# The forget gate's sums in the attention scores: rounded matmuls over 128 rows in place of four-byte matmuls of 8 rows

## The chip, the cores and the metric

The kernel runs on one core of a Trainium2 chip, in one launch. The metric is the time of that launch on the device in microseconds (us); lower is better. Before the change the runs gave 3453.53 us as their median, from 3452.12 to 3457.21 (3 runs).

## The reference

The reference is a block of two layers over 512 tokens of 1024 features: first a mixer with a recurrent unit and a convolutional feed-forward part, then a state space branch, a "forgetting" attention and a feed-forward part that picks 16 of 16384 experts for each of 8 heads and token. Only the attention is touched here:

```
def forgetting_attention(q, k, v, f_logit, f_bias, q_g, k_g):
    q = head_rms_norm(q...); k = head_rms_norm(k...)
    log_f = jax.nn.log_sigmoid((f_logit + f_bias).astype(jnp.float32)).transpose(0, 2, 1)
    cum = jnp.cumsum(log_f, axis=-1)
    ...
        s = jnp.einsum('bhqd,bhkd->bhqk', q_blk, k).astype(jnp.float32) * scale
        s = s + c_blk[..., None] - cum[:, :, None, :]
        s = jnp.where(key_pos[None, :] <= q_pos[:, None], s, -jnp.inf)
        p = jax.nn.softmax(s, axis=-1)
        return jnp.einsum('bhqk,bhkd->bhqd', p.astype(v.dtype), v)
```

There are 8 heads of 128 features and 4 blocks of 128 queries. The term `c_blk` is the same for all keys of a query and drops out of the softmax, so a kernel only has to add `-cum` of the key to each score.

## The kernel before, in words

The program is written engine by engine, and the order on each engine is the order of the code; semaphores tie them together. Every activation lies with features on the 128 partitions and tokens along the columns. Weights stream through a ring of 5 tiles of 128x1024 (`fetch`, on SyncE). A projection is computed with operands in two parts: ScalarE rounds a tile to the type fp32r (`high`, L930), VectorE or GpSimd subtracts to get the rest (`low`, L1310 and L1962), and TensorE runs three rounded matmuls of 512 columns for each of 8 chunks (`three`), 24 in all. An fp32 operand instead makes four-byte matmuls, which the trace shows as two passes each with its own weight load. All matmuls are recorded under the helper line L576, transposes under L837.

The attention part on TensorE: the last two projections of keys, the 8-row projection `f` of the forget gate, the values `vv`, then `scores(0)`, and a loop over heads `hd` = 0 to 7, here called rounds: a projection (`k2` to `k7`, then `ga6`, `ga7`), the transposes of the probabilities, for rounds 0 to 5 a `head_sum` (the sum of squares of the new keys, for their norm), `scores(hd + 1)`, and the product of probabilities and values ("mixing", `probsT,vt`). So `scores` is called 8 times, as call 0 ahead of the loop and as call n in round n - 1.

A call of `scores` handles 4 blocks of queries; block qb has (qb + 1) x 128 keys. Each block is a sum of three products in one bank of PSUM: keys and queries (`kT`, `qT`); `sel` and `cumn`, which adds row hd of the 8x512 sums to all 128 queries; and `ident` and `maskt`, which puts -1e30 above the diagonal of the last 128 columns. All three are four-byte. The lower four banks are used in turn by head sums and score blocks. With five of them in rounds 0 to 5, the last block of a call takes the bank of the head sum in front of it, and waits for ScalarE's square root of that sum (`hsd_done`).

Beside it ScalarE evicts the projection (to `kT` or `gaT`), rounds the next weight tile, squares the keys (`ht`), rounds `mg` of the head before once VectorE has merged it, takes the root of the head sum, computes the exponentials of the four blocks, and evicts the mixed values. VectorE makes the weight tile's low half, merges the head before (L1802, L1803), copies the transposed probabilities `probsT` (L1815), takes the maxima of the score blocks (L1784), norms the new keys (L1703, L1704) and divides the probabilities by their sums (L1791, L1792, "the shares"), which the next round's transposes wait for.

The forget gate's sums are made by VectorE between the `f` projection and the work for `vv` (L1761 to L1771): `cumn` is 8x512. GpSimd builds `sel` (a one in row hd for head hd, 128 columns wide) once the states are done.

Of the kernel before, what the change touches and what calls it, by code (L numbers as in the profile page):

```python
# [15 lines left out]
P = 128  # L16
# [236 lines left out]
def build(nc, io):  # L253
    with ExitStack() as ctx:
# [7 lines left out]
        def sb(name, cols, dt=F32):  # L262
            return ctx.enter_context(nc.sbuf_tensor(name, [P, cols], dt))
# [2 lines left out]
        wh_t, wl_t = sb("wh", RH * D, F32R), sb("wl", RH * D, F32R)  # L266
        vec, mod_t, small = sb("vec", NVEC), sb("mod", 96), sb("small", 1024)
        ones, ident, iota, maskt = sb("ones", P), sb("ident", P), sb("iota", P), sb("mask", P)
        ARENA = 39400
        base = 4 * (-(-nc.sbuf_base // 32) * 8)  # L270
        sb("arena", ARENA)
# [2 lines left out]
        def ar(name, at, chunks, w=T, dt=F32):  # L274

            assert at + chunks * w <= ARENA
            t = nc.alloc_sbuf_tensor_at(name, [P, chunks * w], dt, offset=base + 4 * at)
            return t[:, :].rearrange("p (c w) -> p c w", w=w)
# [67 lines left out]
        gl = ar("gl", B + 20480, 4)  # L346
        kT, vt2 = ar("kT", B, HEADS), ar("vt2", B + 12288, NB, D)
        fl = [ar(f"fl{k}", B + 20480 + k * T, 1)[0:HEADS, 0, :] for k in range(5)]
        sel, cumn = ar("sel", B + 23040, HEADS, P), ar("cumn", B + 24064, 1)[0:HEADS, 0, :]
        probs = [ar(f"probs{k}", B + 20480 + k * (k + 1) // 2 * P, 1, (k + 1) * P)[:, 0, :] for k in range(NB)]  # L350
        probsT = [ar(f"probsT{k}", B + 21760 + (k * NB - k * (k - 1) // 2) * P, 1, (NB - k) * P)[:, 0, :]
                  for k in range(NB)]
# [91 lines left out]
        def _(sp):  # L444
# [6 lines left out]
            def stream(stage, name, n, w=D):  # L451
                for u in range(n):
                    fetch(TILE[f"{stage}{u}"], io[name][u], w)
# [66 lines left out]
                projection(f"k{n}")  # L520
            fetch(TILE["f"], io["w_f"], KD * HEADS)
            stream("vv", "w_v2", 8)
            for name in IN_HEADS:
                projection(name)
            stream("out2_", "w_out2", KD)
# [46 lines left out]
        def _(pe):  # L572
# [244 lines left out]
            def scores(hd):  # L817
                pe.wait_ge(S("qk_normed"), HEADS + hd + 1)
                for qb in range(NB):
                    b, nk = BLOCK[f"scores{hd}"] + qb, (qb + 1) * P  # L820
                    block_free(pe, b)
                    mm(bank(b, nk), qT[:, hd, qb * P:(qb + 1) * P], kT[:, hd, 0:nk], True, False)
                    mm(bank(b, nk), sel[0:HEADS, hd, :], cumn[:, 0:nk], False, False)
                    mm(bank(b)[:, qb * P:nk], ident[:, :], maskt[:, :], False, True).then_inc(PE, 1)

            pe.wait_ge(S("cum_ready"), 1)
            pe.wait_ge(S("mask_ready"), 2)
            scores(0)
            pe.wait_ge(S("v2_read"), 2 * NB)
            for hd in range(HEADS):  # L830
# [468 lines left out]
        def _(ve):  # L1299
# [454 lines left out]
            for n in range(2):  # L1754
# [13 lines left out]
            log1p_exp(fl[1], fl[3], fl[4], fl[3], fl[2])  # L1768
            link(TS(fl[1], fl[0], 0.0, -1.0, ALU.min, ALU.mult))
            link(TT(fl[2], fl[2], fl[1], ALU.add))  # L1770
            v.tensor_tensor_scan(cumn, ones[0:HEADS, 0:1].to_broadcast([HEADS, T]), fl[2], 0.0, ALU.mult, ALU.add)\  # L1771
                .then_inc(S("cum_ready"), 1)
            for n in range(2):
                low_after(TILE[f"vv{n}"])
                head_norm(HEADS + n)
# [167 lines left out]
        def _(gp):  # L1943
# [10 lines left out]
            g.affine_select(out=maskt[:, :], in_=maskt[:, :], compare_op=ALU.is_ge, fill=NEG, base=0,  # L1954
                            pattern=[[-1, P]], channel_multiplier=1).then_inc(S("mask_ready"), 1)

            def low(name):

                e = HALF[TILE[name]]
                wh, wl = whl(e, 0, D)  # L1960
                gp.wait_ge(S("high_ready"), e + 1)
                g.tensor_tensor(wl, slot(WHOLE_OF[e], 0, D), wh.bitcast(F32), ALU.subtract)\  # L1962
                    .then_inc(S("low_by_gp"), 1)
            for name in FFN:
                if name[0] != "d":
                    low(name)

            gp.wait_ge(S("out_done"), NS)
            g.memset(sel, 0.0).then_inc(S("mask_zero"), 1)
            gp.wait_ge(S("mask_zero"), 2)  # L1970
            g.affine_select(out=sel, in_=sel, compare_op=ALU.not_equal, fill=1.0, base=0,
                            pattern=[[-1, HEADS], [0, P]], channel_multiplier=1).then_inc(S("mask_ready"), 1)

            for j in range(PK):
                low(f"ui{j}")
# [123 lines left out]
```

## Time and profile before

| | us |
|---|---|
| median of the runs | 3453.53 |
| the profiled execution | 3455.41 |
| its span, first to last instruction | 3452.9 |
| TensorE matmuls busy | 3306.8 (96%) |
| VectorE busy | 2017.2 (58%) |
| ScalarE busy | 1076.0 (31%) |
| GpSimd busy | 428.3 (12%) |

The granted TensorE clock over the span is 0.98 of full. The chain of work that ended last lies 88% on TensorE and 9% on VectorE.

How to read it: an engine is "busy" from the start to the end of its instructions; those of TensorE overlap, and their ends are modelled, so the distance from one start to the next tells more than a duration. In a timeline a row may stand for several instructions merged ("x2"). The idle time before a row and what ended it stand in brackets. The attention part lies between about 1516 and 1730 us.

### The profile page before, as it was taken

How to read it: one execution, taken by the hardware profiler on the slowest of the kernel's cores; microseconds unless marked ns; L12 is line 12 of the kernel's file. 1: busy time of each engine (PE TensorE's matmuls, PEld its weight loads, DVE VectorE, ACT ScalarE, POOL GpSimd, SP SyncE). 2: the span in 40 equal slices, each digit the busy share in tenths (PEclk: the TensorE clock that was granted, in tenths of full speed). 3: DMA queues.
4: the chain of work that ended last, by engine and by line, in shares of the span. 5: the costliest groups of instructions: out<-in, count | busy, mean ns of one | idle time of the engine just before them, and what ended most of it. 6: DMA issues, size and time to landing. Idle time of an engine off the chain costs nothing.

```text
span 3452.9 us, 37952 instructions
## 1 busy us (share of the span) xinstructions
PE 3306.8 (96%) x14700; PEld 2589.5 (75%) x14700; DVE 2017.2 (58%) x3757; ACT 1076.0 (31%) x1401; POOL 428.3 (12%) x184
## 2 busy tenths in 40 slices
PE   7999889989999699999989999999999999999999
PEld 6776678867777455766568888888888788888887
DVE  5678443347897789644633858676641255555554
ACT  3265222223223222224432333355542211111111
POOL 0000000003132000000001344432334200000000
PEclk9999999999999899999999999999999999999999
DMA  5144214332242333221123344387875555555553
GB/s 187 47 142 128 86 61 139 116 100 80 80 153 75 108 119 107 86 74 55 31 61 95 127 139 140 126 196 185 197 189 195 177 190 187 187 191 184 192 185 116
DMA packets 280946, 451.56 MB, mean 131 GB/s; under 512 B 147776, under 2 KB 154048, under 8 KB 280512
## 3 DMA queue, kind: packets, MB, share of 16 engines
q1 hardware_dynamic: 145152, 405.10, 36.1%
q10 hardware_dynamic: 135616, 44.04, 6.0%
q8 instruction: 117, 1.92, 0.2%
q14 instruction: 61, 0.50, 0.0%
HBM read 369.39 MB, written 79.69 MB: 130 GB/s over the span
## 4 chain that ended last, share of the span: by engine, by line
PE 88%; DVE 9%; ACT 2%; issue 1%; DMA 0%; ACTq 0%; DVEq 0%
PE psum L576 88%; DVE wl L1310 1%; DVE ht L1703 1%; ACT wh L930 1%; DVE st L1712 1%; DVE n L1455 0%; DVE yb L1513 0%; DVE h_lo L1449 0%; DVE trig L1404 0%; DVE lb L1504 0%; DVE st L1719 0%; DVE st L1722 0%; DVE cs L1511 0%; DVE trig L1405 0%; DVE trig L1407 0%
## 5 line engine op out<-in xcount | busy, mean ns | idle before, releaser
L576 PE MATMUL psum<-h_hi,wh 128*128 128x512 f32 x2144 | 872.8, 407 | 44.6 <-DVE h_lo L1449 21.0
L1310 DVE TENSOR_TENSOR wl<-ring,wh 128x1024 fp32r<-128x1024 f32 (+2 forms) x320 | 375.1, 1175 | 887.4 <-ACT wh L930 887.0
L576 PE MATMUL psum<-h_lo,wh 128*128 128x512 f32 x2144 | 850.2, 397 | 0.0
L576 PE MATMUL psum<-h_hi,wl 128*128 128x512 f32 x2144 | 849.9, 396 | 0.0
L930 ACT ACTIVATE wh<-ring 128x1024 fp32r<-128x1024 f32 (+2 forms) x492 | 504.1, 1027 | 851.9 <-PE psum L576 839.1
L1962 POOL TENSOR_TENSOR wl<-ring,wh 128x1024 fp32r<-128x1024 f32 x172 | 424.7, 2470 | 1942.6 <-ACT wh L930 1942.6
L576 PEld LDWEIGHTS psum<-h_hi,wh 128*128 128x128 f32 x2144 | 406.0, 189 | 150.0 <-issue 43.6
L576 PEld LDWEIGHTS psum<-h_hi,wl 128*128 128x128 f32 x2144 | 406.0, 189 | 102.6
L576 PEld LDWEIGHTS psum<-h_lo,wh 128*128 128x128 f32 x2144 | 406.7, 190 | 91.9 <-issue 4.1
L576 PE MATMUL psum<-ews_hi,wh 128*128 128x512 f32 x1024 | 408.7, 399 | 0.7 <-ACT ga L1280 0.7
L576 PE MATMUL psum<-ews_hi,wl 128*128 128x512 f32 x1024 | 403.5, 394 | 0.0
L576 PE MATMUL psum<-ews_lo,wh 128*128 128x512 f32 x1024 | 401.4, 392 | 0.0
L1280 ACT ACTIVATE ga<-psum 128x512 f32<-128x512 f32 x128 | 76.5, 597 | 501.1 <-PE psum L576 501.1
L576 PEld LDWEIGHTS psum<-ews_hi,wl 128*128 128x128 f32 x1024 | 192.2, 188 | 50.1
L576 PEld LDWEIGHTS psum<-ews_lo,wh 128*128 128x128 f32 x1024 | 192.2, 188 | 45.9
L576 PEld LDWEIGHTS psum<-ews_hi,wh 128*128 128x128 f32 x1024 | 192.2, 188 | 45.3 <-ACT ga L1280 1.1
L1905 DVE TENSOR_SCALAR hot_a<-psum,picksT 128x128 f32<-128x128 f32 x512 | 173.8, 401 | 0.0
L1901 DVE TENSOR_TENSOR hot_b<-psum,picksT 128x512 f32<-128x512 f32 x128 | 87.5, 684 | 116.6 <-PE psum L576 116.6
L1646 DVE SCALAR_TENSOR_TENSOR psum<-ffpad,vec,psum 128x512 f32<-128x512 f32 x176 | 133.1, 756 | 6.3
L1916 DVE TENSOR_TENSOR er<-abuf,gbuf 128x512 f32<-128x512 f32 x128 | 90.0, 703 | 70.6 <-DMA gbuf<-gates_scratch 70.6
L1267 ACT ACTIVATE stage<-psum 128x512 f32<-128x512 f32 x128 | 126.1, 1124 | 3.3 <-PE psum L576 2.0
L576 PEld LDWEIGHTS psum<-hot_b,hot_a 128*128 128x128 f32 x1024 | 120.9, 192 | 3.6
(357 smaller groups left out, 3852.3 us busy)
## 6 DMA issues: line engine op xcount, KB each, us to landing
ring<-tables SPq DMA_DIRECT2D x256, 512.0 KB, 3.7
acts_scratch<-ga SPq DMA_DIRECT2D x128, 256.0 KB, 2.2
gates_scratch<-stage ACTq DMA_DIRECT2D x8, 4096.0 KB, 27.1
abuf<-acts_scratch SPq DMA_DIRECT2D x128, 256.0 KB, 3.9
gbuf<-gates_scratch SPq DMA_DIRECT2D x128, 256.0 KB, 4.2
ring<-w_up SPq DMA_DIRECT2D x44, 512.0 KB, 3.6
ring<-w_modb SPq DMA_DIRECT2D x32, 512.0 KB, 3.7
statew<-states_scratch SPq DMA_DIRECT2D x16, 640.0 KB, 3.8
```

The costliest lines, as they stand in the source:

```text
L576: return nc.tensor.matmul(out, lhsT, rhs, start=first, stop=last, **kw)
L930: A(whl(e, 0, size[t])[0], slot(t, 0, size[t]), ACT.Copy).then_inc(S("high_ready"), 1)
L1267: A(parked[g % 2][:, :, t0:t0 + 4].rearrange("p j t -> p t j"), t3(bank(b), P), ACT.Copy)\
L1280: A(ga4[:, j % 4, :], psum[:, 4 + j % 2, :], ACT.Gelu_apprx_tanh).then_inc(S("ea_ready"), 1)
L1310: TT(wl, slot(t, 0, size[t]), wh.bitcast(F32), ALU.subtract).then_inc(S("low_by_ve"), 1)
L1646: step(STT(cv, win, C("fcw", n * 9 + k), cv, ALU.mult, ALU.add))
L1703: link(v.reciprocal(ht[:, 2 + n % 2, :], ht[:, 2 + n % 2, :]))
L1712: TT(st[:, k, :], psum[:, bk, :], tab, ALU.mult).then_inc(S("xs_read"), 1)
L1901: TT(t3(hot_b[:, n % 4, :], P), rows.unsqueeze(1).to_broadcast([P, 4, P]), picksT[:, 1, 4 * n:4 * n + 4].unsqueeze(2).to_broadcast([P, 4, ...
L1905: last = TS(hot_a[:, n % 4, q * P:(q + 1) * P], rows, picksT[:, 0, t:t + 1], picksT[:, 2, t:t + 1], ALU.is_equal, ALU.mult)
L1916: TT(er[:, b % 2, :], abuf[:, b % NV, :], gbuf[:, b % NV, :], ALU.mult).then_inc(S("ew_raw"), 1)
L1962: g.tensor_tensor(wl, slot(WHOLE_OF[e], 0, D), wh.bitcast(F32), ALU.subtract)\
```

## The change

`sel` and the four-byte use of `cumn` go. The 8x512 sums are kept in two rounded parts: `cums` is a tile of 128 rows of which rows 0 to 7 hold the rounded sums and rows 32 to 39 the rounded rest; all other rows are zero. VectorE writes the rounded part and the rest (into `cum_lo`, rows 0 to 7), and a DMA on SyncE moves the rest to rows 32 to 39. The stationary operand is a column of `pick_head`, which has a one in rows hd and 32 + hd, read 128 times over. One rounded matmul then adds both parts. The mask goes through rounded copies of `ident` and `maskt`. The product of keys and queries stays as it is.

```
-        sel, cumn = ar("sel", B + 23040, HEADS, P), ar("cumn", B + 24064, 1)[0:HEADS, 0, :]
+        ident_r, mask_r = sb("ident_r", P, F32R), sb("mask_r", P, F32R)
+        pick_head = sb("pick_head", HEADS, F32R)
+        cums, cum_lo = (ar(name, B + at, 1, T, F32R)[:, 0, :] for name, at in (("cums", 23040), ("cum_lo", 23552)))
+        cumn = ar("cumn", B + 24064, 1)[0:HEADS, 0, :]
...  (SyncE, behind the fetches of w_v2)
             stream("vv", "w_v2", 8)
+            sp.wait_ge(S("cum_ready"), 1)
+            sp.dma_start(cums[32:32 + HEADS, :].bitcast(F32), cum_lo[0:HEADS, :].bitcast(F32)).then_inc(S("cum_moved"), 16)
...  (TensorE, scores)
                     mm(bank(b, nk), qT[:, hd, qb * P:(qb + 1) * P], kT[:, hd, 0:nk], True, False)
-                    mm(bank(b, nk), sel[0:HEADS, hd, :], cumn[:, 0:nk], False, False)
-                    mm(bank(b)[:, qb * P:nk], ident[:, :], maskt[:, :], False, True).then_inc(PE, 1)
-
-            pe.wait_ge(S("cum_ready"), 1)
-            pe.wait_ge(S("mask_ready"), 2)
+                    mm(bank(b, nk), pick_head[:, hd:hd + 1].to_broadcast([P, P]), cums[:, 0:nk], False, False)
+                    mm(bank(b)[:, qb * P:nk], ident_r[:, :], mask_r[:, :], False, True).then_inc(PE, 1)
+
+            pe.wait_ge(S("cum_moved"), 16)
+            pe.wait_ge(S("mask_ready"), 4)
             scores(0)
...  (VectorE, after the scan's input)
-            v.tensor_tensor_scan(cumn, ones[0:HEADS, 0:1].to_broadcast([HEADS, T]), fl[2], 0.0, ALU.mult, ALU.add)\
-                .then_inc(S("cum_ready"), 1)
+            link(v.tensor_tensor_scan(cumn, ones[0:HEADS, 0:1].to_broadcast([HEADS, T]), fl[2], 0.0, ALU.mult, ALU.add))
+            ve.wait_ge(S("cum_zero"), 1)
+            link(v.tensor_copy(cums[0:HEADS, :], cumn))
+            TT(cum_lo[0:HEADS, :], cumn, cums[0:HEADS, :].bitcast(F32), ALU.subtract).then_inc(S("cum_ready"), 1)
...  (GpSimd, at the start)
+            gp.wait_ge(S("consts_ready"), 4)
+            gp.wait_ge(S("mask_ready"), 1)
+            g.tensor_copy(mask_r[:, :], maskt[:, :]).then_inc(S("mask_ready"), 1)
+            g.tensor_copy(ident_r[:, :], ident[:, :]).then_inc(S("mask_ready"), 1)
+            g.tensor_tensor(pick_head[:, :], ident[:, 0:HEADS], ident[:, 32:32 + HEADS], ALU.add)\
+                .then_inc(S("mask_ready"), 1)
...  (GpSimd, behind out_done)
-            g.memset(sel, 0.0).then_inc(S("mask_zero"), 1)
-            gp.wait_ge(S("mask_zero"), 2)
-            g.affine_select(out=sel, in_=sel, compare_op=ALU.not_equal, fill=1.0, base=0,
-                            pattern=[[-1, HEADS], [0, P]], channel_multiplier=1).then_inc(S("mask_ready"), 1)
+            g.memset(cums.bitcast(F32), 0.0).then_inc(S("cum_zero"), 1)
```

On TensorE the order stays, with other operands. This is one call of `scores` in a round of the changed kernel, with the semaphores that each row waits for:

```order
L581 MATMUL psum<-ht,ones 128x512 [waits hsq_ready,p_exp]
L581 MATMUL psum<-kT,qT 128x128 [waits p_exp,qk_normed]
L581 MATMUL psum<-cums,pick_head 128x128
L581 MATMUL psum<-mask_r,ident_r 128x128
L581 MATMUL psum<-kT,qT 128x256 [waits p_exp]
L581 MATMUL psum<-cums,pick_head 128x256
L581 MATMUL psum<-mask_r,ident_r 128x128
L581 MATMUL psum<-kT,qT 128x384 [waits p_exp]
L581 MATMUL psum<-cums,pick_head 128x384
L581 MATMUL psum<-mask_r,ident_r 128x128
L581 MATMUL psum<-kT,qT 128x512 [waits hsd_done]
L581 MATMUL psum<-cums,pick_head 128x512
```

Each pair of `cums` and `mask_r` stands where `cumn` and `mask` stood; the waits are those of before.

On SyncE, the queue around the fetches of the values' weights, before:

```order
L449 DMA ring<-w_f 128x64 [waits low_by_ve]
L449 DMA ring<-w_v 128x1024 [waits low_by_ve] x4
L449 DMA ring<-w_v 128x1024 [waits pe_done]
L449 DMA ring<-w_v 128x1024 [waits low_by_ve] x3
L449 DMA ring<-w_k 128x1024 [waits low_by_ve] x6
```

and of the changed kernel:

```order
L452 DMA ring<-w_f 128x64 [waits low_by_ve]
L452 DMA ring<-w_v 128x1024 [waits low_by_ve] x4
L452 DMA ring<-w_v 128x1024 [waits pe_done]
L452 DMA ring<-w_v 128x1024 [waits low_by_ve] x3
L527 DMA cums<-cum_lo 8x512 [waits cum_ready]
L452 DMA ring<-w_k 128x1024 [waits low_by_ve] x6
```

The move of the rest stands ahead of the fetches of the keys' weights.

## Rows read from the trace of the kernel before

**Rows 1.** The page: an engine's busy us, share of the span, instructions

```profile
PE 3306.8 (96%) x14700; PEld 2589.5 (75%) x14700; DVE 2017.2 (58%) x3757; ACT 1076.0 (31%) x1401; POOL 428.3 (12%) x184
```

**Rows 2.** The chain that ended last: start, us, TensorE's piece in two rounds

```profile
1668.57 17.32 PE psum L576 x58
1688.12 15.64 PE psum L576 x58
```

**Rows 3.** By tile, `cumn`: ns min/median/max, first and last start, forms

```profile
L576 PE MATMUL psum<-cumn,sel x64: 270/480/692, 1581.1 to 1710.6; 8*128 8x128 f32 x16, 8*128 8x256 f32 x16, 8*128 8x384 f32 x16, 8*128 8x512 f32 x16
```

**Rows 4.** Timeline of call 1 on TensorE: start, us, engine, line, operation

```profile
1598.06 0.39 PE L576 MATMUL psum<-kT,qT 128*128 128x128 f32 x2
...
1603.45 1.12 PE L576 MATMUL psum<-cumn,sel 8*128 8x512 f32 x2
1604.50 0.49 PE L576 MATMUL psum<-mask,ident 128*128 128x128 f32 x2
1604.82 2.32 PE L576 MATMUL psum<-probsT,vt 128*128 128x512 f32 x8
```

**Rows 5.** Timeline of round 1, all engines; idle time in brackets

```profile
1612.58 1.25 PE L837 MATMUL psum<-ident,probs 128*128 128x128 f32 x10
...
1614.98 1.10 PE L576 MATMUL psum<-ht,ones 128*128 128x512 f32 x2 [1.15 <-ACT ht L1164]
...
1615.91 0.39 PE L576 MATMUL psum<-kT,qT 128*128 128x128 f32 x2
...
1616.94 1.69 DVE L1815 COPY probsT<-psum 128x512 f32<-128x512 f32 x4
...
1618.88 0.69 ACT L1150 ACTIVATE ht<-psum,vec 128x512 f32<-128x512 f32 x1
...
1620.35 1.02 PE L576 MATMUL psum<-kT,qT 128*128 128x512 f32 x2
...
1622.68 2.32 PE L576 MATMUL psum<-probsT,vt 128*128 128x512 f32 x8
...
1629.10 0.49 DVE L1792 TENSOR_SCALAR probs<-probs,small 128x512 f32<-128x512 f32 x1
```

**Rows 6.** Timeline of an early projection on TensorE, 512 and 256 columns

```profile
102.18 0.39 PE L576 MATMUL psum<-h_lo,wh 128*128 128x512 f32 x1
...
102.65 0.28 PE L576 MATMUL psum<-hc_hi,wh 128*128 128x256 f32 x1
102.77 0.28 PE L576 MATMUL psum<-hc_lo,wh 128*128 128x256 f32 x1
```

**Rows 7.** Timeline around call 0: TensorE, then ScalarE

```profile
1580.80 0.38 PE L576 MATMUL psum<-kT,qT 128*128 128x128 f32 x2
...
1587.61 0.77 PE L576 MATMUL psum<-h_hi,wh 128*128 128x512 f32 x1
...
1594.72 1.25 PE L837 MATMUL psum<-ident,probs 128*128 128x128 f32 x10
...
1582.02 2.04 ACT L1215 ACTIVATE vt<-psum 128x512 f32<-128x512 f32 x4
```

**Rows 8.** Stretches: busy us (count) of five engines, then clock, DMA, GB/s

```profile
1555.00:1580.50 25.50, 22.35 (x96) 17.98 (x96) 5.75 (x5) 6.18 (x8) 0.00 (x0) 1.00 0.33 102
...
1587.50:1591.00 3.50, 3.50 (x11) 2.78 (x11) 2.52 (x9) 0.78 (x2) 0.00 (x0) 0.53 0.00 0
1675.00:1680.00 5.00, 5.00 (x11) 2.55 (x12) 3.32 (x2) 1.73 (x6) 0.00 (x0) 0.66 0.00 0
```

**Rows 9.** Timeline of round 6: VectorE and TensorE

```profile
1707.96 1.68 DVE L1815 COPY probsT<-psum 128x512 f32<-128x512 f32 x4
...
1711.45 2.32 PE L576 MATMUL psum<-probsT,vt 128*128 128x512 f32 x8
```

**Rows 10.** Timeline of VectorE around the gate's sums

```profile
1542.43 0.68 DVE L1770 TENSOR_TENSOR fl<-fl,fl 8x512 f32<-8x512 f32 x1
...
1544.29 1.19 DVE L1310 TENSOR_TENSOR wl<-ring,wh 128x1024 fp32r<-128x1024 f32 x1
```

## The prediction

> **What bounds the kernel now.** I read the busy shares first: TensorE is busy for 3306.8 us, 96% of the span [rows 1]. Anything on TensorE that is not covered by a wait elsewhere is time. Then the stretch of the change: the attention part calls `scores` eight times, once in front of the loop over heads and once inside each of its first seven rounds. The rows by tile show that the sums of the forget gate run as 64 matmuls with an 8-row stationary operand, two passes for each of 32 matmuls [rows 3]; the mask has as many. The timeline of one `scores` call shows what they take [rows 4]: it runs from 1598.06 to 1604.82, 6.76 us. In its last block of 512 columns the sums take 1603.45 to 1604.50 = 1.05 us and the mask 1604.50 to 1604.82 = 0.32 us. Last the timeline of one round [rows 5], to see which wait comes last there, and the granted clock [rows 8].
>
> **The matmuls, one call.** Four blocks of 128, 256, 384 and 512 columns, each with three products. The product of keys and queries stays four-byte. Its columns are those of the `probsT,vt` matmuls, also four-byte with 128 rows: two passes over 1280 columns in 2.32 us [rows 4], whose last one is drawn some 0.2 us long past the next start. So 1.2 columns per ns, 2 x 1280 / 1.2 = 2.13 us. Within the call now it takes more: sums in proportion to 1.05 us (two passes, plus about 0.2 us of weight loads that start only with the matmul) come to 0.41 + 0.63 + 0.84 + 1.05 = 2.93 us, the mask to 4 x 0.32 = 1.28 us, so 6.76 - 4.21 = 2.55 us is left for keys and queries. I take the difference of 0.42 us for the cost of switching between 8 and 128 rows, and let it go.
>
> The rounded form's cost is read from the projections [rows 6]: two products of 512 columns take 102.65 - 102.18 = 0.47 us, 0.235 each, one of 256 columns 0.12 us, one pass. 384 columns lie between, 0.18. 128 columns in this form are in no row. Below stands 128 / 512 of 0.235, 0.06; above, the two passes of the mask now, 0.32. Nearest are ten transposes of 128 columns with a load each, 1.25 us in all, at most 0.125 each [rows 5]. I take 128 / 1.2 = 0.107, a load's time at that pace. Sums: 0.11 + 0.12 + 0.18 + 0.23 = 0.64. Mask: 0.43. The call comes to 2.13 + 0.64 + 0.43 = 3.2 us, 3.5 less than now. If the loads stay exposed and the 128-column products cost twice my value, it is 2.55 + 0.75 + 0.86 = 4.2 us, 2.6 less. Four bytes of `cums` in 128 rows instead of 8 cost TensorE nothing by columns. The stationary operand of the sums reads one column 128 times over; no row shows such a load. From below it costs what other loads do; from above I allow one pass more per product, which the 4.2 us holds in part.
>
> **Where the gain is let through.** *Call 0, ahead of the loop* [rows 7]: starts at 1580.80, would end at 1584.0. The projection behind it waits for ScalarE's four copies of `vt`, 1582.02 + 2.04 = 1584.06. It starts at about 1584.2 in place of 1587.61: 3.4 us.
>
> *Call 1, in round 0*: nothing waits inside (round 0 has no merge of a head before, so ScalarE's root of the head sum comes some 2 us earlier than in a later round), so 3.5 us.
>
> *Calls 2 to 6, in rounds 1 to 5* [rows 5]: here a new wait appears. The head sum and the four score blocks use four banks, so that the last block needs the bank of the head sum in front of it, and waits for `hsd_done`, ScalarE's root of that sum. That root is at 1618.88 + 0.69 = 1619.57 and stands behind a copy that waits for VectorE's merge, so it hangs on the start of the round and not on the scores. Now TensorE comes to the last block at 1620.35, later than the root. After, the first three blocks take 2.0 us from 1615.91, to 1617.9, and TensorE waits to about 1619.7 (the root and some 0.1 us for the signal). The last block takes 0.853 + 0.234 + 0.107 = 1.2 us: end 1620.9 to 1621.0 in place of 1622.68, 1.7 us a round, 5 x 1.7 = 8.5 us. Half of the saved work turns into that wait. It also covers dear small products in the first three blocks, up to 1.8 us.
>
> Does another wait come late next? The mixing product wants `probsT`, whose copies start at 1616.94 and take 1.69: there before 1619. The next round's transposes want the shares, now at 1629.10 + 0.49 = 1629.59, against their turn one round after 1612.58, at 1612.58 + (1612.58 - 1594.72) = 1630.44 [rows 5, 7]: 0.85 us to spare. That VectorE chain (last maximum, norm of the keys, the shares) starts from the last score block, and moves earlier by the same 1.7 us, so the 0.85 us stay.
>
> *Call 7, in round 6* [rows 9]: no head sum, no such wait. The call ends at 1711.45 - 3.5 = 1707.95, but `probsT` is copied only from 1707.96 on; its first copy is out near 1708.6. Gain 1711.45 - 1708.6 = 2.85 us. Round 7 has no scores, and its waits follow the end of its projection, so nothing is given back.
>
> Sum: 3.4 + 3.5 + 8.5 + 2.85 = 18.2 us.
>
> **The clock.** Twice in this part the granted clock falls to its lower level, 1.2 of 2.4 GHz, while TensorE is busy all the time: 0.53 in 1587.5 to 1591, behind call 0, and 0.66 in 1675 to 1680, in a round [rows 8]. Both follow `scores`. A wait of 3.15 us in the stretch from 1555 left it at 1.00 [rows 8]. The projection behind call 0 took 1594.72 - 1587.61 = 7.1 us against 24 x 0.235 = 5.6 at full clock, 1.5 us more; the round took 17.32 against 15.64 in its sister at 1688.12 [rows 2], 1.7 us more. What goes away is 8-row work, what comes is work on 128 rows and 1.8 us of waiting a round, less than the 3.15 us that the clock bore. I expect both drops to go: 3.2 us, and 0 to 3.2 as bounds, with up to 3 lost instead if the new waits bring drops.
> The Trainium skill's "TensorE: Matmul & The Clock Gate" (Part 1, what is actually happening) puts a drop down to idle time of TensorE. The trace does not bear that out for these two, where it was busy throughout. By that rule the change removes no cause and adds waits, so the sum would stay at 18.2 us or less; this is the second case below.
>
> **What lies beside other work.** VectorE gets a copy and a subtraction of 8x512, at most 0.68 us each as the addition of that shape, and a few hundredths between [rows 10]. Queued behind them is the low half for a weight tile three ahead, at 1544.29, which TensorE reaches two projections later; a shift of 1.4 us is hidden by the projections in between (5.6 us each), and if it were not it would cost at most that. The sums' low part then moves by DMA to rows 32 to 39, 16 KB. SyncE waits for `cum_ready` before it; behind stands the fetch of the next `w_k` tile, which waits for the low half that VectorE makes after the sums anyway. The transfer has from about 1546 to 1580.80 to land, so TensorE's wait for it is free; a move that took 50 us would cost some 16. GpSimd has three small operations at the start and later one memset in place of two operations, all far from use.
>
> **Sum.** 18.2 + 3.2 = 21.4 us. The profiled execution took 3455.4 us, 1.9 more than the median of the runs, 3453.53. That gives 3434.0, or 3432.1 against the median; I say 3433.
>
> **Rivals.**
> 1. The clock drops stay, or the new waits make others: 18.2 less, 3436 (down to 3439 with more drops). For: drops come and go with phase, and only two of eight calls had one. Against: both stood behind work that goes. Chance 0.25.
> 2. Dear small products: the call saves only 2.6 us. Calls 0, 1 and 7 lose 0.9 each (call 7 0.3), rounds 1 to 5 about 0.3 each, 3.6 in sum: 3437. For: 128 columns in this form are in no row. Against: one pass cannot well cost what two do. Chance 0.12.
> 3. The wait for the head sum's root does not bind (TensorE's bank is free earlier than I read): rounds 1 to 5 give 3.5 each, 9 more, 3424. For: nothing in a row, as it doesn't wait now. Against: the wait stands in the order, and the root's time is in the trace. Chance 0.04.
> 4. Slower: going over between four-byte and rounded products, or the load of a repeated column beside it, stops TensorE for p us. There are 8 changes of form in a call, 64 in all. In rounds 1 to 5 the wait swallows 1.8 us of the six ahead of the last block. Cost: 64 p - 5 x 1.8. It decides from (21.4 + 9) / 64 = 0.48 us each; at 0.6 us it is 3434 + 29.4 = 3463. For: no row has such a sequence. Against: the score call at 1580.80 and the transposes at 1612.58 are four-byte work straight behind rounded projections, with no idle time ahead of them [rows 5, 7]. Chance 0.04.
> 5. The change does not do what it says: with a four-byte product in the same sum, the rounded ones run at four-byte pace. Only the exposed loads go, 0 to 3 us: 3453. Against: the form is the operands' own, as in the projections. Chance 0.05.
>
> The forecast itself has 0.50 and runs from 3429 to 3435.5. Over all cases the range is 3427 to 3441. A difference under 0.2%, 7 us, can hardly be told from none: faster 0.91, same 0.05, slower 0.04.
>
> **What would show it.** `cums,pick_head` once for each block, 0.23 us apart at 512 columns; calls of about 3.2 us; a TensorE wait of 1.8 us on ScalarE's root before the last block of calls 2 to 6 and none in the others; rounds of about 16.1 us; clock 1.00 through the part. Calls over 4.5 us, a wait for `cum_moved`, or transposes waiting for the shares would make it wrong.

## The result and the profile after

| | before | changed |
|---|---|---|
| median of the runs, us | 3455.33 (3452.12 to 3457.21, 4 runs) | 3425.61 (3424.03 to 3427.22, 4 runs) |
| profiled execution, us | 3455.41 | 3424.04 |
| its span, us | 3452.9 | 3422.1 |

The changed kernel takes 0.9915 of the time before, 95% interval 0.9898 to 0.9932: 29.7 us less. The forecast was 3433, with 3427 to 3441 as its range, so the kernel came out 1.4 us below the range's lower end. (The median before is over one run more than the 3453.53 that the forecast started from.) The direction and the work on TensorE were right; the sum lacked some 8 us.

The page of the changed kernel, its line of the engines [rows 1]:

```profile
PE 3267.0 (95%) x14636; PEld 2587.9 (76%) x14636; DVE 2018.4 (59%) x3759; ACT 1076.3 (31%) x1401; POOL 429.2 (13%) x186
```

64 matmuls are gone: 32 passes of the sums and 32 of the mask. The rows by tile, `cums`, with ns min/median/max [rows 3, 10]:

```profile
L581 PEld LDWEIGHTS psum<-cums,pick_head x32: 190/190/192, 1577.1 to 1684.4; 128*128 128x128 f32 x32
L581 PE MATMUL psum<-cums,pick_head x32: 305/550/800, 1577.1 to 1684.4; 128*128 128x128 f32 x8, 128*128 128x256 f32 x8, 128*128 128x384 f32 x8, 128*128 128x512 f32 x8
...
L1778 DVE CAST cums<-cumn x1: 415/415/415, 1538.0 to 1538.0; 8x512 fp32r<-8x512 f32 x1
L1779 DVE TENSOR_TENSOR cum_lo<-cumn,cums x1: 679/679/679, 1538.4 to 1538.4; 8x512 fp32r<-8x512 f32 x1
L527 SPq DMA_DIRECT2D cums<-cum_lo x1: 759/759/759, 1539.2 to 1539.2; - x1
```

One pass for each block, and the load of a column read 128 times over takes 190 ns, as those of `probsT,vt` do. VectorE's two new instructions take 1.1 us; the move to rows 32 to 39 was issued at 1539.2, long before its use at 1577.

The timeline of call 1 on TensorE, after [rows 4]:

```profile
1589.29 0.38 PE L581 MATMUL psum<-kT,qT 128*128 128x128 f32 x2
...
1591.28 1.07 PE L581 MATMUL psum<-kT,qT 128*128 128x512 f32 x2
1591.79 0.80 PE L581 MATMUL psum<-cums,pick_head 128*128 128x512 f32 x1
1592.43 0.22 PE L581 MATMUL psum<-mask_r,ident_r 128*128 128x128 f32 x1
1592.48 1.07 PE L581 MATMUL psum<-probsT,vt 128*128 128x512 f32 x2
```

The call takes 1592.48 - 1589.29 = 3.19 us in place of 6.76. (Single rows inside it can't be added up: their ends are modelled, and starts follow them.)

The timeline of round 1, after [rows 5]:

```profile
1600.27 1.25 PE L842 MATMUL psum<-ident,probs 128*128 128x128 f32 x10
...
1603.91 0.69 DVE L1810 SCALAR_TENSOR_TENSOR mg<-mg,gaT 128x512 f32<-128x512 f32 x1
...
1604.64 0.63 ACT L1240 ACTIVATE mg_hi<-mg 128x512 fp32r<-128x512 f32 x1 [2.10 <-DVE mg L1810]
...
1605.29 1.28 ACT L1155 ACT_TABLE_LOAD   x1
...
1606.58 0.69 ACT L1155 ACTIVATE ht<-psum,vec 128x512 f32<-128x512 f32 x1
...
1607.32 1.12 PE L581 MATMUL psum<-kT,qT 128*128 128x512 f32 x2 [1.56 <-ACT ht L1155]
...
1608.58 2.37 PE L581 MATMUL psum<-probsT,vt 128*128 128x512 f32 x8
```

The new wait stands before the last block of the call, for ScalarE's root of the head sum, and in front of the root stand a table load of 1.28 us and the copy that waits for VectorE's merge. The chain that ended last now runs through it, in each of rounds 1 to 5:

```profile
1603.91 0.71 DVE mg L1810
1604.66 0.09 issue
1604.77 0.52 issue
1605.29 1.28 ACT L1155
1606.58 0.70 ACT ht L1155
1607.28 0.04 issue
1607.32 9.23 PE psum L581 x36
```

**Where the time went.** Turns, that is the starts of `ident,probs` of a round, put against those of before:

| stretch | before, us | after, us | gain | forecast |
|---|---|---|---|---|
| up to call 0's start | 1580.80 | 1576.95 | 3.85 | 0 |
| call 0 and the projection behind it | 13.92 | 9.00 | 4.92 | 4.9 |
| round 0 | 17.86 | 14.32 | 3.54 | 3.5 |
| rounds 1, 2, 3, 5 | 17.86 each | 16.11 each | 1.75 each | 1.7 each |
| round 4 | 19.55 | 16.11 | 3.44 | 3.4 |
| round 6 | 15.61 | 13.01 | 2.60 | 2.85 |
| behind the last turn | 1733.7 | 1728.3 | 5.4 | 0 |

From call 0 to the last turn the kernel gained 21.5 us; the forecast for it was 21.4. All that it missed, 9.3 us of the two profiled executions, lies outside: the early and late stages hold no changed instruction of TensorE, and yet they were faster. The stretch 2600 to 3300 of both, filled by the experts' matmuls (busy us and count of TensorE, weight loads, VectorE, ScalarE, GpSimd, then clock, DMA share, GB/s); before:

```profile
2600.00:3300.00 700.00, 699.31 (x2997) 562.27 (x2996) 311.85 (x421) 144.18 (x149) 50.52 (x21) 1.00 0.56 186
```

and after:

```profile
2600.00:3300.00 700.00, 699.31 (x3009) 566.68 (x3009) 328.98 (x442) 141.89 (x144) 39.13 (x17) 1.00 0.56 189
```

Both at full clock, with no idle time to speak of, and 12 matmuls more after. From start to start a rounded matmul of 512 columns takes 233.33 ns before and 232.38 after (mean over the experts' stages). What differs for them is where their tiles lie: the three new tiles hold 264 words in each partition, and stand ahead of the arena in which all activations lie, so it moved by 1056 bytes. (Words here are 4 bytes, and all shifts are in each partition.) The kernel has 11,040 such matmuls, 4128 of them ahead of 1550 us and some 6600 behind the attention part; 0.95 ns each would be 10.5 us, 3.9 ahead and 6.3 behind.

### The profile page after: what moved, and what is told of

Its sections match the earlier page's. It is cut to its first block, busy times and chain, and to the rows that moved or that the text cites. A ratio compares the mean times of both kernels' runs of the same rounds, so it can differ in the third digit from the quotient of the medians.

```text
span 3422.1 us, 37830 instructions
## 1 busy us (share of the span) xinstructions
PE 3267.0 (95%) x14636; PEld 2587.9 (76%) x14636; DVE 2018.4 (59%) x3759; ACT 1076.3 (31%) x1401; POOL 429.2 (13%) x186
## 4 chain that ended last, share of the span: by engine, by line
PE 87%; DVE 9%; ACT 2%; issue 1%; DMA 0%; ACTq 0%; DVEq 0%
PE psum L581 87%; DVE wl L1315 1%; ACT wh L935 1%; DVE ht L1708 1%; DVE st L1717 1%; DVE n L1460 0%; DVE yb L1518 0%; DVE h_lo L1454 0%; DVE trig L1409 0%; DVE lb L1509 0%; DVE st L1724 0%; DVE st L1727 0%; DVE cs L1516 0%; DVE trig L1412 0%; DVE trig L1410 0%
```

## The experiments

Kernels that ran together share runs of the kernel before, whose median lay between 3455.1 and 3456.0. Ratios are against it.

### The place of the arena

**1 and 2. The kernel before, its arena moved by 264 words, and by 8.**

```
+        sb("unused", 264)          # in the second: 8
         sb("arena", ARENA)
```

> The kernel before with one unused tile of 264 words a partition ahead of the arena, which is what the three new tiles of the change take: the arena starts 1056 bytes later, nothing else changes. Theory PLACE (the rounded matmuls' pace hangs on where their operands in the arena start; 233.3 ns a piece before and 232.4 after in the expert stage): this kernel shows the 232.4 ns and is some 9 us faster than the kernel before, near 3446. Rival RUN (the pace is of the execution or the chip, not of the program): no change from the kernel before, 3455.

> The kernel before with an unused tile of 8 words (32 bytes) ahead of the arena. By the sizes of the tiles the arena starts at 32 bytes past a multiple of 64 before, and at a multiple of 64 after the change (1056 = 16 x 64 + 32). Theory PLACE in the form 'it is the 64-byte phase': the same 9 us as with 264 words, near 3446, at 232.4 ns. If PLACE holds in another form (a bank, a larger distance), this kernel stays at 3455 while the one with 264 words moves. Theory RUN: 3455 for both.

Measured: 3445.00 us (0.9968, interval 0.9956 to 0.9981) and 3443.46 (0.9964, 0.9950 to 0.9977), both at 232.38 ns. An unused tile ahead of the arena is worth 10 to 12 us, and 32 bytes do as much as 1056. 1056 is 32 more than a multiple of 128.

**3. The changed kernel, its arena moved by 8 words more.**

> The changed kernel with an unused tile of 8 words (32 bytes) ahead of the arena, which puts it back to 32 bytes past a multiple of 64. Theory PLACE by the 64-byte phase: the rounded matmuls go back to 233.3 ns and the kernel loses some 9 us, 3434 to 3435. Theory RUN: 3425.6 as the changed kernel.

Measured: 3444.62 (0.9966, 0.9952 to 0.9980): 19 us slower than the changed kernel, 10 slower than I expected. The same stretch has 24 matmuls fewer than in the changed kernel, 234.28 ns each:

```profile
2600.00:3300.00 700.00, 699.31 (x2985) 562.21 (x2985) 319.66 (x430) 141.72 (x145) 45.22 (x19) 1.00 0.55 186
```

Theory PLACE in its 64-byte form fell with that: there are not two paces but three at least.

**4. The changed kernel with its three tiles behind the arena.** The arena lies where it lay before.

```
-        ident_r, mask_r = sb("ident_r", P, F32R), sb("mask_r", P, F32R)
-        pick_head = sb("pick_head", HEADS, F32R)
         ARENA = 39400
...
         sb("arena", ARENA)
+        ident_r, mask_r = sb("ident_r", P, F32R), sb("mask_r", P, F32R)
+        pick_head = sb("pick_head", HEADS, F32R)
```

> The changed kernel with its three new tiles behind the arena instead of ahead of it, so that the arena starts where it did before: the change of the matmuls alone. Theory PLACE, in any form: 3434, which is the kernel before less the 21.4 us of the prediction's sum. Theory RUN: 3425.6.

Measured: 3433.41 (3433.11 to 3433.68; 0.9935, 0.9922 to 0.9949), with rounds of 14.32, 16.11 five times, 13.04:

```profile
2600.00:3300.00 700.00, 699.31 (x2998) 562.27 (x2997) 324.73 (x436) 142.30 (x145) 41.72 (x18) 1.00 0.56 187
```

This is the change alone, at the pace of before, and what the forecast of 3433 spoke of.

**9, 10, 13 and 14. Which shift sets the pace.** 9: the kernel before, arena moved by 16 words. 10: the changed kernel, arena moved by 16 words more. 13: the kernel before, 8 unused words ahead of all tiles, so that weights and arena move by 32 bytes together. 14: weights moved by 32 bytes and the arena by 128.

```
+        sb("unused", 8)            # 13 and 14, ahead of wh and wl
         wh_t, wl_t = sb("wh", RH * D, F32R), sb("wl", RH * D, F32R)
...
+        sb("unused2", 24)          # 14
         sb("arena", ARENA)
```

> The kernel before with an unused tile of 16 words (64 bytes) ahead of the arena. So far the rounded matmuls of the expert stage ran at 233.3 ns with the arena in the old place, 232.4 at +32 and +1056 bytes, 234.3 at +1088. Theory PHASE128 (the pace hangs on the arena's start modulo 128 bytes, as 1056 = 8 x 128 + 32 and 1088 = 8 x 128 + 64): +64 bytes runs like +1088, 234.3 ns, and is as much slower as the changed kernel was between those places (3444.6 - 3433.4 = 11.2 us): 3466. Rival DISTANCE (1088 bytes moved something by its size, not by its phase): 3455 or 3445.

> The changed kernel with 16 unused words ahead of the arena: it starts 1120 = 8 x 128 + 96 bytes past the old place, the fourth phase of 32 bytes. Theory PHASE128 says that it has a pace of its own, and not which. By the three known (0: 233.3, 32: 232.4, 64: 234.3 ns) I expect it between the two neighbours 64 and 0, 233.3 to 234.3 ns: 3433 to 3445. Rival, the 64-byte phase counts in part: 232.4 ns as at 32, 3425.6.

> The kernel before with 8 unused words (32 bytes) ahead of all its tiles: the weights' ring, the rounded weights wh and wl, and the arena with the moving operands all start 32 bytes later. Theory MOVING (the pace hangs on where the moving operand in the arena starts, absolutely): as with the arena alone 32 bytes later, 232.4 ns and 3443.5. Theory RELATIVE (it hangs on the distance of the two operands, which stays): 233.3 ns and 3455. A third pace would say that both places count.

> The kernel before with 8 unused words ahead of all tiles and 24 more ahead of the arena: ring, wh and wl start 32 bytes later, the arena 128 bytes later, which is its old phase. Theory MOVING: 233.3 ns and 3455, as before. Theory RELATIVE: the distance changes by -32 modulo 128, as with the arena at +96 alone: 233.3 ns by that kernel too, so here the two agree; theory STATIONARY (the weights' place counts): another pace, and a time that differs by 5 us or more.

Measured, ordered by the arena's shift less that of the weights, modulo 128 bytes. This is the distance of the two operands counted from the kernel before, where it is called 0. (The ns are means from start to start over the experts' stages.)

| distance | kernel | weights, arena moved (bytes) | ns | time, us | ratio (interval) |
|---|---|---|---|---|---|
| 0 | before | 0, 0 | 233.33 | 3455.33 | |
| 0 | 13 | 32, 32 | 233.33 | 3454.69 | 1.0001 (0.9992 to 1.0010) |
| 0 | 4 | 0, 0 | 233.34 | 3433.41 | 0.9935 (0.9922 to 0.9949) |
| 32 | 1, 2 | 0, 1056 / 0, 32 | 232.38 | 3445.00 / 3443.46 | 0.9968 / 0.9964 |
| 32 | changed | 0, 1056 | 232.38 | 3425.61 | 0.9915 (0.9898 to 0.9932) |
| 64 | 9 | 0, 64 | 234.28 | 3462.74 | 1.0020 (1.0011 to 1.0029) |
| 64 | 3 | 0, 1088 | 234.28 | 3444.62 | 0.9966 (0.9952 to 0.9980) |
| 96 | 10 | 0, 1120 | 233.33 | 3433.31 | 0.9935 (0.9922 to 0.9949) |
| 96 | 14 | 32, 128 | 233.33 | 3453.24 | 0.9994 (0.9985 to 1.0003) |

Experiment 13 moved the arena by the 32 bytes that gave experiment 2 its 12 us, and gained nothing: it is not the place of the arena alone. In 14 the arena has moved by a full 128 bytes and the weights by 32. By the mean, 233.33 ns, it can't be told from the kernel before; but its matmuls are evenly spaced (233.3 ns each) like those of 10, and not like those of before, 13 and 4, where the three products of a chunk take 237.5, 230.9 and 231.6 ns. What all ten kernels agree with is the distance between the two operands, modulo 128 bytes; weights moved by other than 0 and 32 bytes were not tried. The mechanism behind it stays open.

Experiment 9 had the pace that I expected, but not the time: 3462.74 in place of 3466, 7 us above the kernel before for 0.95 ns, where 3 against 4 was 11. The time depends on the clock too: the stretches at 1.2 GHz fall differently in each of these kernels. So the pace is reproduced to 0.01 ns, the time that it costs only within some us.

### The sums, the mask, rows and passes

**5 and 6. One half of the change each.** 5 is the changed kernel with the four-byte mask. 6 is the kernel before with the rounded mask, and with the three tiles ahead of the arena.

```
-                    mm(bank(b)[:, qb * P:nk], ident_r[:, :], mask_r[:, :], False, True).then_inc(PE, 1)    # 5
+                    mm(bank(b)[:, qb * P:nk], ident[:, :], maskt[:, :], False, True).then_inc(PE, 1)
...
-                    mm(bank(b)[:, qb * P:nk], ident[:, :], maskt[:, :], False, True).then_inc(PE, 1)       # 6
+                    mm(bank(b)[:, qb * P:nk], ident_r[:, :], mask_r[:, :], False, True).then_inc(PE, 1)
```

> The changed kernel, but the mask stays a four-byte product (two passes on 128 rows). Theory WORK (the prediction's sum: a call of scores is the sum of its passes, and calls 2 to 6 wait for ScalarE's root): a call takes 3.2 + 4 x 0.107 = 3.6 us; calls 0, 1 and 7 lose 0.4 each, of calls 2 to 6 only the last mask counts, 0.1 each: 3425.6 + 1.8 = 3427.5. Rival MASK (the mask product itself carries a large part of the gain, by its 0.32 us in the kernel before): 32 x 0.26 = 8 us lost, 3434.

> The changed kernel's mask alone: the sums are the four-byte product of 8 rows again (no rounded sums, no move by DMA), with the arena where the changed kernel has it. To be compared with the kernel before at that place, 3445.0. Theory WORK: a call goes from 6.76 to 5.9 us, 8 x 0.85 = 6.8 us less: 3438. Theory CLOCK (8-row work brings the drops of TensorE's clock in this part, 3.2 us): one or two drops to the lower level behind a call of scores, as in the kernel before; rival: drops come by chance of phase, and this profile may have none.

**7. Rows without rounding.** The kernel before with the four-byte sums in a zeroed tile of 128 rows, and a column of `ident` read 128 times over. Still two passes each; the mask stays four-byte, and the three tiles lie ahead of the arena, as in 5 and 6.

```
-                    mm(bank(b, nk), sel[0:HEADS, hd, :], cumn[:, 0:nk], False, False)
+                    mm(bank(b, nk), ident[:, hd:hd + 1].to_broadcast([P, P]), cums[:, 0:nk], False, False)
```

> No rounded product at all in scores: the sums stay four-byte but stand in rows 0 to 7 of a zeroed tile of 128 rows, with a column of the identity read 128 times over as the stationary operand; the mask is the four-byte one. It tells what the 8 rows cost apart from the passes. Theory WORK: the passes alone are 2.13 + 2.13 + 0.85 = 5.1 us a call, 1.65 less than 6.76, if the switching between 8 and 128 rows was the exposed weight loads; calls 0, 1, 7 gain 1.65 each, calls 2 to 6 about 1.1 each (they begin to wait for the root): 10.4 us, and with the clock's 3.2 it is 3445.0 - 13.6 = 3431. Rival: the rows cost nothing, the weight loads stay exposed: a call stays at 6.7 us and the kernel at 3445 (3442 if the clock's drops go).

| | call 1, us | undisturbed rounds 1 to 5, us | time, us | ratio (interval) |
|---|---|---|---|---|
| arena alone (1) | 6.76 (before) | 17.83 | 3445.00 | 0.9968 (0.9956 to 0.9981) |
| mask (6) | 6.27 | 17.40 | 3451.66 | 0.9992 (0.9983 to 1.0001) |
| 128 rows (7) | 5.20 | 16.83 | 3436.47 | 0.9942 (0.9928 to 0.9956) |
| sums (5) | 3.68 | 16.20 | 3426.14 | 0.9916 (0.9902 to 0.9930) |
| both (changed) | 3.19 | 16.11 | 3425.61 | 0.9915 (0.9898 to 0.9932) |

The sums save 3.08 us of a call and the mask 0.49, with or without the other. Experiment 5 was expected at 3427.5 by theory WORK and came within 1.4 us, and rival MASK, 3434, fell. Of the sums' part, 1.56 us is not arithmetic at all: experiment 7 has the passes and columns of before, and differs in rows (and in the stationary operand, a repeated column). Its call runs without a gap, here the last block, and one weight load:

```profile
1599.18 1.02 PE L578 MATMUL psum<-kT,qT 128*128 128x512 f32 x2
1600.05 1.02 PE L578 MATMUL psum<-cums,ident 128*128 128x512 f32 x2
1600.90 0.38 PE L578 MATMUL psum<-mask,ident 128*128 128x128 f32 x2
1601.12 0.59 PE L578 MATMUL psum<-probsT,vt 128*128 128x512 f32 x1
...
1600.48 0.19 PEld L578 LDWEIGHTS psum<-mask,ident 128*128 128x128 f32 x1 [0.24 <-issue]
```

512 four-byte columns take 0.87 and 0.85 us from start to start, keys and sums alike, and the mask 0.22; in the kernel with 8 rows (here experiment 6) they take 1.01 and 1.05, and the mask of before took 0.32 [rows 4]:

```profile
1597.47 1.07 PE L578 MATMUL psum<-kT,qT 128*128 128x512 f32 x2
1598.48 1.12 PE L578 MATMUL psum<-cumn,sel 8*128 8x512 f32 x2
1599.53 0.33 PE L578 MATMUL psum<-mask_r,ident_r 128*128 128x128 f32 x1
```

So the keys' product and the mask beside an 8-row product pay too, though they have not changed: weight loads that are covered among 128-row products lie open at the changes of rows. In experiment 7 the mask's load starts at 1600.48, a pass ahead of its matmul at 1600.90. In the kernel before the same load of the same tile, behind the 8-row pass, starts only with its matmul at 1604.50 [rows 4]:

```profile
1604.50 0.30 PEld L576 LDWEIGHTS psum<-mask,ident 128*128 128x128 f32 x2 [0.76 <-issue]
```

Experiment 7 also has a repeated column where the kernel before has `sel`, a full tile. That is not what opens the loads: in the kernel before the load of `probsT`, a full tile too, behind the mask's 128 rows starts at 1604.71, ahead of its matmul at 1604.82.

Experiment 7 as a whole was expected at 3431 and measured 3436.47. That sum was wrong in one term: it started from experiment 1's 3445.00 and took off 3.2 us for clock drops, which experiment 1 doesn't have from call 0 to the end of round 6. Without it the expectation is 3434.6.

On top of the sums the mask gives the whole kernel nothing that could be measured (3426.14 against 3425.61). In the traces it gives 0.3 us at call 0, 0.4 in round 0 and 0.09 in each of rounds 1 to 5, where the wait for the root takes the rest: 1.2 us. A clock drop in round 7 that is 3.4 us shorter in experiment 5 can hide them.

In experiment 6 the work saved did not show in the time: 3451.66, where 3438 was expected. What it saves by its trace, 0.43 us a round and 3 us in all, should have given 3442 on top of experiment 1. Its granted clock says why (columns as above):

```profile
1617.20:1620.60 3.40, 3.40 (x7) 1.67 (x7) 3.30 (x2) 0.86 (x3) 0.00 (x0) 0.50 0.00 0
1651.30:1661.50 10.20, 10.20 (x18) 5.08 (x19) 6.12 (x9) 3.81 (x10) 0.00 (x0) 0.50 0.00 0
1705.90:1716.10 10.20, 10.20 (x18) 5.00 (x18) 5.32 (x17) 3.00 (x10) 0.00 (x0) 0.50 0.09 35
```

23.8 us at 1.2 GHz, with TensorE busy throughout, cost about half of that: the three rounds took 19.08, 22.29 and 20.03 us.

### What binds next

**8, 11 and 12. The root's wait, then the shares.** 8: the changed kernel with ScalarE's root ahead of the copy that waits for VectorE's merge. 11: 8, and the square of the new keys ahead of the rounding of the weight tile. 12: 11, and on VectorE the weight tile's low half behind the copies of `probsT`.

```
+                if hd + 2 < HEADS:                # 8: ahead of the copy of mg
+                    head_root(HEADS + hd + 2)
...
-                if hd + 2 < HEADS:                # its place before
-                    head_root(HEADS + hd + 2)
...
+                if upper_bank:                    # 11: behind the square of the new keys
+                    high_after(TILE[name])
...
+                low_after(TILE[IN_HEADS[hd]])     # 12: behind the copies of probsT
```

> The changed kernel with ScalarE's root of the head sum put ahead of its rounding of mg (which waits for VectorE's merge) in each round. Theory WORK (the last score block of calls 2 to 6 waits 1.6 us for that root): the wait goes, rounds 1 to 5 take 14.4 instead of 16.1 us, 8 us less: 3417 to 3418. Rival SHARES: VectorE's chain to the probabilities' shares becomes the last wait of a round, as it has only 0.85 us to spare: 4 us less at most, 3421 or above.

> The changed kernel with ScalarE's root ahead of the rounding of mg, and also its square of the new keys ahead of the rounding of the next weight tile. With the root first, rounds 1 to 6 take 14.31 us, TensorE waits 1.15 us for the square in each, and the shares are ready 0.05 us ahead of the transposes. Theory SHARES (VectorE's chain is next: it starts with the low half of the weight tile, which now comes 0.6 us later, and ends in the shares): transposes wait about 1 us for the shares, which the vanished wait for the square pays: rounds of 13.9 to 14.0, 2 us less than root first, 3413. Rival WORK alone (only TensorE's work counts): rounds of 13.2, 3408.

> As the kernel with root and square first, and VectorE makes the low half of the weight tile after its copies of probsT instead of at the start of the round. VectorE then starts on the merge at once and is done with the shares some 12.6 us after the projection's end. Theory SHARES: that chain is no longer last, a round is TensorE's work of 13.0 us and 0.3 us of waiting for the square: 13.3 us, 6 us less than root first alone, 3409. Rival: another wait comes up (the copies for the transposes, or ScalarE's order): 14 us or more, 3413.

| | rounds 0 to 6, us | time, us | ratio (interval) |
|---|---|---|---|
| changed | 14.32, 16.11 x5, 13.01 | 3425.61 | 0.9915 (0.9898 to 0.9932) |
| 8 | 14.31 in each of 0 to 5 | 3414.78 | 0.9885 (0.9869 to 0.9901) |
| 11 | 13.50, 14.98, 13.69, 14.27, 13.70, 14.27, 12.12 | 3413.94 | 0.9879 (0.9863 to 0.9894) |
| 12 | 13.51 x6, 12.09 | 3405.14 | 0.9852 (0.9838 to 0.9865) |

In 8 the root starts 3.57 us into the round in place of 6.31, and the wait before the last block is gone. The shares are now ready only 0.05 us ahead of the transposes, whose first load waits for them:

```profile
1603.49 0.69 ACT L1155 ACTIVATE ht<-psum,vec 128x512 f32<-128x512 f32 x1
1604.28 0.63 ACT L1242 ACTIVATE mg_hi<-mg 128x512 fp32r<-128x512 f32 x1
...
1613.70 0.49 DVE L1799 TENSOR_SCALAR probs<-probs,small 128x512 f32<-128x512 f32 x1
1614.24 0.86 PEld L842 LDWEIGHTS psum<-ident,probs 128*128 128x128 f32 x8 [0.29 <-DVE probs L1799]
```

The time, 3414.78, is 10.8 us below the changed kernel, where theory WORK had 8 and rival SHARES at most 4: the rounds give 9.0 by the traces, and a clock drop in round 7 that is 3.4 us shorter can give the rest.

In 11 TensorE waits for the shares for up to 1.13 us. Its rounds take 2.3 us less than those of 8 in sum (2 were expected), but the times, 3413.94 and 3414.78, are too close to be told apart:

```profile
1616.78 1.31 PE L842 MATMUL psum<-ident,probs 128*128 128x128 f32 x10 [1.13 <-DVE probs L1802]
```

In 12 it no longer does. VectorE copies `probsT` before it makes the low half:

```profile
1601.91 1.25 PE L842 MATMUL psum<-ident,probs 128*128 128x128 f32 x10
...
1602.64 1.69 DVE L1824 COPY probsT<-psum 128x512 f32<-128x512 f32 x4 [0.28 <-PE psum L842]
...
1604.35 1.23 DVE L1318 TENSOR_TENSOR wl<-ring,wh 128x1024 fp32r<-128x1024 f32 x1
...
1615.42 1.25 PE L842 MATMUL psum<-ident,probs 128*128 128x128 f32 x10
```

TensorE is then busy for 98% of the attention part, at full clock:

```profile
1576.00:1706.00 130.00, 127.58 (x579) 96.24 (x578) 97.64 (x180) 70.60 (x132) 0.00 (x0) 1.00 0.17 49
```

Experiment 12 is the fastest kernel of the study, 20.5 us below the changed one and 4 us below what was expected. Rounds 0 to 6 give 14.8 us of it (13.51 us each, 13.3 expected). The rest comes from a wait that no theory here had: in round 7 the mixing product waits 3.95 us for `probsT`, whose copies stand on VectorE behind the low half and the merge. In the changed kernel:

```profile
1699.03 4.61 PE L581 MATMUL psum<-probsT,vt 128*128 128x512 f32 x8 [3.95 <-DVE probsT L1822]
```

and in 12:

```profile
1683.17 2.40 PE L581 MATMUL psum<-probsT,vt 128*128 128x512 f32 x8 [0.32 <-DVE probsT L1824]
```

With that wait the clock drop of round 7 is gone too; by the two profiles they are worth 3.6 us and, by estimate, 2.7 (the drop covers 5.5 us of work in the changed kernel). In the two profiles 12 is 2.4 us later than the changed kernel at the first turn, which takes part of it back.

## Why the prediction was wrong, and where it was right

- **The term that was missing: the place of the new tiles.** The step of the prediction that failed is its sum, 18.2 + 3.2 us: it counted instructions, waits and clock inside the attention part, put everything outside at nothing, and has no word on where the new tiles lie. The diff shows the three tiles allocated ahead of the arena, and I passed over it. Their 1056 bytes change the distance between the operands of all rounded projections by 32 modulo 128 bytes, and with it the time of each of them: 232.38 ns in place of 233.33. Taken away (experiment 4), the change gives 3433.41 against the forecast of 3433: the 7.8 us between experiment 4 and the changed kernel are the miss of 7.4.
- **The size of that term.** 7.8 us between experiment 4 and the changed kernel, 10.3 and 11.9 in experiments 1 and 2, 11.3 between 3 and 10, 7 in experiment 9, each for about 0.95 ns a matmul, which by the count of matmuls is 10.5 us. They differ because clock drops elsewhere come and go. In the profiles the changed kernel gains 6.5 us up to 1548, of which the pace explains 3.9 and fewer drops can explain the rest; it then loses 2.6 ahead of call 0 to a drop that the kernel before doesn't have. From 1830 us on it gains 6.3 us, evenly, all of it by the pace. So the size of 7.8 us is the pace's 10.5 less what the drops happened to take.
- **The matmuls of a call**: 3.2 us forecast, 3.19 measured, and the price of each product after the change holds. What was misread is which product the time of before belongs to. Replaced alone, the mask saves 0.49 us and not 0.85, the sums 3.08 and not 2.29. I had seen 0.2 us of open load in each sums' product, 0.8 in all, and left 0.42 of keys and queries unexplained. With 0.1 us in each mask, which I took for the mask's own, these make 1.6 us, the 1.56 of experiment 7. All of it goes with the 8 rows. The forecast of the call is right because all three products were priced without open loads; a forecast for one half of the change would have been off by 0.4 to 0.8 us a call. The rounded product of 128 columns is near the 0.107 that I took (a four-byte mask at 0.22 less 0.12), and rival 2 fell.
- **The root's wait** (rounds 1 to 5): the place was right, before the last block of calls 2 to 6. It lasts 1.56 us against 1.8, and the round gains 1.75 against 1.7. Experiment 8 takes it away and the round loses 1.80 more, so rival 3 fell.
- **The transposes' spare time**: 0.85 us forecast, and in the changed kernel the shares end 0.88 us before the next turn (1615.50 against 1616.38). In experiment 8, with a round 1.8 us shorter, it was 0.05 us: the chain to the shares does not move along with the scores any further, and is the next to bind.
- **Call 7**: 2.60 against 2.85. TensorE waits 0.76 us for the first copy of `probsT`, as said, somewhat longer than said.
- **The clock, 3.2 us**: the two drops went, and with them the 3.2 us, and the new waits of 1.56 us brought no others, so rival 1 fell. But one argument for it was unsound. I took a wait of 3.15 us that left the clock at 1.00 [rows 8] as proof that waits below it are harmless. The same wait, in the changed kernel:

```profile
1545.00:1550.80 5.80, 3.57 (x16) 2.54 (x14) 5.76 (x5) 2.13 (x4) 0.00 (x0) 1.00 0.23 90
1550.80:1557.60 6.80, 5.87 (x14) 4.62 (x15) 0.97 (x1) 0.87 (x2) 0.00 (x0) 0.51 0.48 154
```

  from 1548.6 to 1551.73 nothing runs on TensorE, and the clock falls to 1.2 GHz for 6.8 us. In experiments 4 and 13 it is there and the clock stays. Of the 16 profiles, all with this wait, 13 have the drop. Whether such a wait brings one changes from kernel to kernel, and the forecast had no term for this one, 2.6 us lost, which the larger gain by the pace hides. The wait of 3.95 us in round 7 has a drop in it, or within 1.2 us of its end, in 15 profiles of 15; in experiment 12, without the wait, there is none.

  The other argument, that 8-row work goes, is borne out by the count. From call 0 to the end of round 6 the seven profiles with 8-row products have 10 drops (before 2, experiment 1 none, 2 one, 6 three, 9 one, 13 two, 14 one), the nine with 128 rows none (changed, 3, 4, 5, 7, 8, 10, 11, 12), and 7 among them does the four-byte passes of before. Each of the ten begins inside a call of `scores` or within 0.1 us of its end, though the calls fill only 6.76 of a round's 17.86 us. The Trainium skill's "TensorE: Matmul & The Clock Gate" (Part 1, what is actually happening) puts drops down to idle time: the drop at 1550.8 agrees, and so do those of round 7; those of the 8-row calls, at a busy TensorE, do not. Why the one 8-row profile has none, and what sets where the others fall, stays open.
- **Form changes, repeated column, one pass** (rivals 4 and 5): nothing of either; the loads of the repeated column take 190 ns and each product one pass.

## What to carry to other kernels

A change also moves what it doesn't touch: when a tile is added, put it behind the others or move them by an unused tile, and compare the start-to-start time of the matmuls in a stage that has no changed instruction, before a gain or loss is put down to the edit. A wait that is forecast to swallow half of a gain is the next edit: here moving the root, the square and one low half, with no work removed, gave 20.5 us, nearly as much again as the change itself (21.9, experiment 4), some 3 of them by a clock drop that went with a wait.

## What the runs showed of the hardware

- In ten kernels the pace of rounded matmuls of 512 columns goes with how far the distance of their two operands in a partition was shifted against the kernel before, modulo 128 bytes: 232.38 ns at 32, 233.33 at 0 and 96, 234.28 at 64. Of this kernel 0.95 ns a matmul was 7 to 12 us.
- Four-byte products of 8 rows among those of 128 rows cost 1.56 us a call in weight loads that lie open; as zero-padded 128 rows the same passes run without gaps, at 0.85 to 0.87 us for 512 columns.
- TensorE's clock fell to 1.2 GHz for 3.4 or 10.2 us while it was busy, 10 times in 7 profiles, each time from within an 8-row call or 0.1 us behind it, and never in 9 profiles with 128-row calls. That the 8 rows are the cause is not shown beyond this count.
- A wait of TensorE of 3.15 us was followed by a drop in 13 of 16 profiles, one of 3.95 us in 15 of 15.
- A stationary operand that is one column read 128 times over loads in 190 ns, as the loads of `probsT,vt` do.
